# A two-layer encoder trunk: the norms ahead of four matrix products made token tile by token tile

## The reference

```python
def rmsnorm(x, g):
    y = xf * lax.rsqrt(jnp.mean(xf * xf, axis=-1, keepdims=True) + EPS)
    return (y * g.astype(jnp.float32)).astype(x.dtype)
...
    for i in range(DEPTH):
        if i % N_MIXERS == 0:
            x = x + mlstm_mixer(x, *mix_params[i])
        else:
            lambda_init = 0.8 - 0.6 * math.exp(-0.3 * i)
            x = x + diff_attn_mixer(x, positions, *mix_params[i], lambda_init=lambda_init)
        x = x + peer_ffn(x, *ffn_params[i])
```

## Time and profile before

| | |
|---|---|
| median of 3 runs | 1866.83 us (1865.65 to 1868.53) |
| the profiled execution | 1865.97 us, span of its instructions 1864.2 us |
| busy in the span | PE 1847.5 us (99%), DVE 1420.9 (76%), ACT 974.8 (52%), POOL 105.8 (6%) |
| chain that ended last | PE 95%, DVE 3%, ACT 1% |

### The profile page before, as it was taken

How to read it: one execution, slowest core, us unless ns; L and a number is a source line. 1 busy time by engine, 2 the same in 40 slices (tenths; PEclk the granted TensorE clock), 3 DMA queues, 4 the chain that set the end, 5 groups by cost and what they waited for, 6 DMA issues and landing times.

```text
span 1864.2 us, 32895 instructions
## 1 busy us (share of the span) xinstructions
PE 1847.5 (99%) x11242; PEld 1554.4 (83%) x11242; DVE 1420.9 (76%) x2599; ACT 974.8 (52%) x1394; POOL 105.8 (6%) x71
## 2 busy tenths in 40 slices
PE   8999999999999999999999999999999999999999
PEld 6778888888888888888887788888888888888887
DVE  5576688988888888655588757889888888885555
ACT  5475555654545444444467645565545544444443
POOL 0000341000000000000000014410000000000000
PEclk9999999999999999999999999999999999999999
DMA  6345555555555555555553355555555555556555
GB/s 231 135 136 160 162 187 191 181 172 170 167 177 172 180 177 170 193 187 195 192 185 119 115 181 170 182 179 183 180 175 172 180 169 173 176 172 194 198 190 171
DMA packets 89487, 326.15 MB, mean 175 GB/s; under 512 B 10064, under 2 KB 10192, under 8 KB 89040
## 3 DMA queue, kind: packets, MB, share of 16 engines
q1 hardware_dynamic: 88848, 323.00, 53.1%
q10 hardware_dynamic: 576, 2.33, 0.3%
HBM read 324.24 MB, written 1.05 MB: 174 GB/s over the span
## 4 chain that ended last, share of the span: by engine, by line
PE 95%; DVE 3%; ACT 1%; issue 0%; DMA 0%; ACTq 0%; DVEq 0%
PE ps L1531 25%; PE ps L1529 14%; PE ps L1776 13%; PE ps L1778 12%; PE ps L1777 12%; PE ps L1528 4%; PE ps L1724 3%; PE ps L1548 2%; PE ps L1550 2%; PE ps L1549 2%; DVE wl L848 1%; PE ps L1705 1%; PE ps L1668 1%; PE ps L1831 0%; PE ps L1861 0%
## 5 line engine op out<-in xcount | busy, mean ns | idle before, releaser
L848 DVE TENSOR_TENSOR wl<-raw,wh 128x1024 fp32r<-128x1024 f32 x569 | 697.1, 1228 | 158.4 <-ACT wh L477 149.6
L477 ACT ACTIVATE wh<-raw 128x1024 fp32r<-128x1024 f32 x609 | 641.7, 1055 | 312.3 <-PE ps L1778 164.9
L1531 PE MATMUL ps<-hT,wh 128*128 128x512 f32 x2072 | 739.3, 396 | 0.0
L1529 PE MATMUL ps<-hT,wl 128*128 128x256 f32 x2368 | 613.1, 279 | 0.0
L1529 PEld LDWEIGHTS ps<-hT,wl 128*128 128x128 f32 x2368 | 446.6, 189 | 25.1
L1531 PEld LDWEIGHTS ps<-hT,wh 128*128 128x128 f32 x2072 | 389.7, 188 | 79.4
L1776 PE MATMUL ps<-wh,hT 128*128 128x512 f32 x1024 | 402.1, 393 | 0.3 <-DVE big L832 0.2
L1778 PE MATMUL ps<-wh,hT 128*128 128x512 f32 x1024 | 399.2, 390 | 0.0
L1777 PE MATMUL ps<-wl,hT 128*128 128x512 f32 x1024 | 398.6, 389 | 0.0
L1778 PEld LDWEIGHTS ps<-wh,hT 128*128 128x128 f32 x1024 | 192.3, 188 | 40.6
L1776 PEld LDWEIGHTS ps<-wh,hT 128*128 128x128 f32 x1024 | 192.4, 188 | 39.5 <-issue 0.9
(11 more groups left out here) (226 smaller groups left out, 1327.2 us busy)
## 6 DMA issues: line engine op xcount, KB each, us to landing
raw<-stream SPq DMA_DIRECT2D x612, 512.0 KB, 3.5
big<-keys ACTq DMA_DIRECT2D x2, 1024.0 KB, 8.6
x<-x_in SPq DMA_DIRECT2D x1, 1024.0 KB, 5.6
out<-x SPq DMA_DIRECT2D x4, 256.0 KB, 2.1
sm<-small ACTq DMA_DIRECT2D x1, 228.5 KB, 5.8
pos_i<-positions ACTq DMA_DIRECT2D x1, 1.0 KB, 6.7
```

The costliest lines, as they stand in the source:

```text
L477: act.activation(wh[:, r, :], raw[:, r, :], ACT.Copy).then_inc(high_ready, 1)
L848: dve.tensor_tensor(wl[:, r, :], raw[:, r, :], wh[:, r, :].bitcast(F32), ALU.subtract).then_inc(made_low(unit), 1)
L1529: pe.matmul(near, w_l[:, kd, :], hTh[:, kd, :], start=False, stop=False)
L1531: i = pe.matmul(wide, w_h[:, kd, :], both, start=False, stop=(kd == KD - 1))
```

## The change

Five things are changed, the first four in all norms or in those with n > 0.

1. Variance, root and reciprocal are made for each token tile apart, and DVE's adds to x are put between them: both quarters of tile 0, its variance, one quarter of tile 1, reciprocal of tile 0, the other quarter, scaling of tile 0, then tile 1.
2. PE transposes all 8 blocks of tile 0, then all of tile 1, into 4 banks with two blocks in each: blocks kd and kd + 4 share a bank. For tile 1 the transpose of blocks 4 to 7 waits until DVE has made `hTl` of block kd - 4, and ACT's copy of these blocks has the same wait.
3. The warming matmuls ahead of the transposes (10, 16, 10) go; 5 come between the two token tiles for n = 2, 3, 5.
4. Before the feed-forward norms ACT and DVE issue one high and one low part less (`U_WO - 2` for `U_WO - 1`); they come behind the norm.
5. In the loop over 16 softmax steps DVE's call of `ahead` is left out for the last step.

```diff
-        TURN_BANK = {0: (7, 4, 5, 6, 0, 1, 2, 3), 2: (4, 5, 6, 7, 0, 1, 2, 3), 3: (4, 5, 6, 7, 0, 1, 2, 3),
-                     5: (4, 5, 6, 7, 0, 1, 2, 3)}
+        TURN_BANK = {0: (4, 5, 6, 0), 2: (2, 3, 0, 5), 3: (6, 7, 0, 1), 5: (5, 6, 7, 2)}
...
+                def root(t):
+                    act.wait_ge(var_ready, 2 * k + t + 1)
+                    act.activation(rstd[:, t:t + 1], var[:, t:t + 1], ACT.Sqrt).then_inc(std_ready, 1)
...
+                    if i == (2 if n == 0 else 1):
+                        root(0)
+                root(1)
...
+                    if kd >= 4:
+                        act.wait_ge(hT_ready, 8 * n + kd - 3)
...
-            ahead(unit_of["wo0"] + U_WO - 1)
+            ahead(unit_of["wo0"] + U_WO - 2)
...
+            def norm(n, k, add=lambda t, nb: None):
...
+                add(0, 0)
+                add(0, 1)
+                variance(0)
+                add(1, 0)
+                factor(0)
+                add(1, 1)
+                scaled(0)
+                variance(1)
+                factor(1)
+                scaled(1)
...
-                ahead(unit_of["qkv"] + 15 + STEP_AT[j] // 4)
+                if j < 15:
+                    ahead(unit_of["qkv"] + 15 + STEP_AT[j] // 4)
...
-                for kd in range(KD):
-                    for t in range(NT):
+                for t in range(NT):
+                    if t == 1 and n > 0:
+                        keep_warm(4, 5)
+                    for kd in range(KD):
                         if kd in (0, KD // 2):
-                            pe.wait_ge(xn_ready, 4 * XN_TURN[n] + 2 * (kd // 4) + t + 1)
-                        i = pe.transpose(ps[:, TURN_BANK[n][kd], t * P:(t + 1) * P], xn[:, t, kd * P:(kd + 1) * P],
+                            pe.wait_ge(xn_ready, 4 * XN_TURN[n] + 2 * t + kd // 4 + 1)
+                        if t == 1 and kd >= 4:
+                            pe.wait_ge(hT_ready, 8 * n + kd - 3)
...
             def ffn(l):
-                keep_warm(4, 10)
                 transposes((2, 5)[l])
...
-            keep_warm(4, 16)
             transposes(3)
```

More of the change, by code:

```diff
@@ L812, in chain, with variance, factor, scaled @@
                 dve.wait_ge(dve_step, steps[0])
[L814 to L821, removed]
-                    for t in range(NT):
+            def norm(n, k, add=lambda t, nb: None):
+                def variance(t):
+                    dve.wait_ge(ssq_ready, 4 * k + 2 * t + 2)
+                    dve.scalar_tensor_tensor(out=var[:, t:t + 1], in0=ssq[:, t, 0:1], scalar=EPS, in1=ssq[:, t, 1:2],
+                                             op0=ALU.add, op1=ALU.add).then_inc(var_ready, 1)
+                def factor(t):
+                    dve.wait_ge(std_ready, 2 * k + t + 1)
+                    chain(dve.reciprocal(var[:, t:t + 1], rstd[:, t:t + 1]))
+                def scaled(t):
+                    for nb in range(2):
                         half = slice(nb * 512, (nb + 1) * 512)
@@ L864, in gain, with add_to_x @@
                 return lambda kd: sm[:, SM_GAIN + g * KD + kd:SM_GAIN + g * KD + kd + 1]
[L866 to L872, removed]
+            def add_to_x(l, t, nb):
+                last = unit_of[f"wo{l}"] + U_WO - 2 + nb
+                if t == 0:
+                    ahead(unit_of[f"wo{l}"] + U_WO - 2)
+                    dve.wait_ge(wo_mm, 2 * l + nb + 1)
+                else:
+                    dve.wait_ge(used, last + 1)
+                dve.tensor_tensor(x[:, t, nb * 512:(nb + 1) * 512], x[:, t, nb * 512:(nb + 1) * 512],
+                                  ps[:, OUT_BANKS[l][nb] + t, :], ALU.add).then_inc(x_ready, 1)
             def head_var(part, k, scale, eps=None):
@@ L1534, in up_both_halves, with token_half @@
                 i.then_inc(used, 1)
+            def token_half(w, q, t, out, between=lambda t, k: None):
+                w_h, w_l = (v.rearrange("p (k c) -> p k c", k=2) for v in w)
+                for k in range(2):
+                    kd = 2 * q + k
+                    between(t, k)
+                    if t == 0:
+                        tokens_ready(kd)
+                    h_h, h_l = hTh[:, kd, t * P:(t + 1) * P], hTl[:, kd, t * P:(t + 1) * P]
+                    pe.matmul(out, h_h, w_h[:, k, :], start=(kd == 0), stop=False)
+                    pe.matmul(out, h_h, w_l[:, k, :], start=False, stop=False)
+                    i = pe.matmul(out, h_l, w_h[:, k, :], start=False, stop=(kd == KD - 1))
+                return i
             def token_unit(unit, q, out, done, before=lambda t: None, between=lambda t, k: None):
-                w_h, w_l = (w.rearrange("p (k c) -> p k c", k=2) for w in split(unit))
+                w = split(unit)
                 for t in range(NT):
@@ L1541, in token_unit @@
                         before(t)
[L1542 to L1550, removed]
+                    i = token_half(w, q, t, out(t), between)
                     if q == 3 and t == 0:
@@ L1555, in out_projection @@
             def out_projection(l, n, ready):
-                for q in range(4):
+                first = unit_of[f"wo{l}"]
+                for q in range(3):
                     for nb in range(2):
@@ L1781, in down @@
+                        i = down_half(w, r, t, turn is None and r == 0)
                     i.then_inc(used, 1)
```

81 lines of the change are left out of this document (43 added, 38 removed).

## The result

The changed kernel takes 1878.04 us (median of four runs, 1874.13 to 1880.37) beside 1867.09 us for the kernel before (1865.65 to 1868.53). The ratio is 1.0056, with a 95% interval of 1.0042 to 1.0070: it is slower, by some 10.5 us (the medians differ by 10.95; the ratio is not exactly their quotient). The profiled execution is the quickest of the four, 1874.13 us with a span of 1872.2 us, 8.0 us longer than the span of before. This difference between executions, 6 us from the quickest to the slowest, is a part of the answer.

The account below looks back on a forecast made before the run. PE, busy in 99% of the span, was taken as the bound. Terms 0.3 + 1.8 + 3.2 + 1.8 = 7.1 us, plus 1.7 for one clock fall, gave 8.8 us of loss: 1875.6 us, range 1870.5 to 1881.5.

Parts of the forecast that it names:

- the forecast: Main case, 60%: gaps at the norms as worked out, none or one clock fall; 1875.6 us, own range 1872.5 to 1878.5.
- the first rival: Clock falls at two or three of n = 2, 3, 5, staying low through the first query unit: 10.5 to 14.3 us; 27%.
- The sum at full clock: Losses at the four norms added together with the clock at full speed: 7.1 us.
- n = 2: Hand-over at this norm: late second tile and waiting transposes, first query matmul at 144.06; +1.8 us.
- n = 3: Hand-over at this norm: waits plus a low part between hTl blocks, first matmul at 945.07; +3.2 us.
- n = 5: Hand-over at this norm: the same picture as n = 2; +1.8 us.
- n = 0: Norm at the start: hTl hardly moves (12.2), high and low parts come later; +0.3 us.
- The waits: Second tile's transposes of blocks 4 to 7 wait for hTl of blocks 0 to 3, delaying the first matmul after each norm.
- the rival that they are cheap: Copies run ahead of the transposes, so blocks 4 to 7 find their bank free: 3.1 us, 1870; 10%.
- The clock: PE's clock falls to half speed behind the new gaps at n = 2, 3, 5: one fall of three, +1.7 us.
- The last high and low part: Deferred behind the feed-forward norms, ready at about 147.2 before PE wants them at 149.7: no cost.
- The softmax step's call: Call left out at the last of 16 softmax steps asks only for units already requested: 0 us.

Follow-up runs that it names:

- e1: Changed kernel with ten warming matmuls put back ahead of the first transpose of n = 2, 3 and 5: 1874.13 us, 1.0050 of before.
- e9: The changed kernel measured once more, with nothing altered: 1878.96 us, 1.0066 of before.
- e10: Changed kernel with warming put back, plus warming in the holes of n = 2, 3 and 5 and five matmuls at n = 0: 1873.58 us, 1.0034.
- e3: Changed kernel with warming put back, eight banks and no waits for hTl; warming between tiles kept in unused half-banks: 1868.23 us, 1.0015.
- e5: Changed kernel with warming put back ahead of tile 0, eight banks, no waits and no warming between the token tiles: 1.0003 of before.
- e8: Kernel before with n = 0 tile by tile, 12 warming matmuls for 16 at n = 3, last high/low part deferred: 1865.47 us, 0.9994.
- e6: Changed kernel with warming put back, plus warming matmuls in the holes between waiting transposes at n = 2, 3 and 5: 1.0032 of before.
- e7: Changed kernel with warming put back, and at n = 3 DVE's low parts moved behind all eight hTl: 1871.10 us, 1.0027.
- e4: Kernel before with only the four shared banks and the waits for hTl added, at all four norms: 1872.69 us, 1.0046.
- e2: Kernel before without its 10, 16 and 10 warming matmuls, nothing else changed: 1871.21 us, 1.0039.

## Why the prediction came out as it did

The direction was right, and the time lies within the range: 1875.6 us forecast, 1878.04 measured, 8.8 us of loss forecast and some 10.5 measured. It is even within the forecast's own range (1872.5 to 1878.5), by 0.5 us; that is in part luck, since the number of falls was the first rival's and the rest of the loss came out a little under the sum.

**The sum at full clock** (7.1 us) holds within a microsecond or so. With the holes filled the kernel is 1.0032 and 1.0034 of before, 6.0 and 6.3 us (5.05 and 6.35 by the medians). By place: n = 2 1.80 us for 1.8, with the first query matmul at 143.85 for 144.06, in a hand-over that began 0.16 sooner; n = 3 8.17 less 5.13, 3.0 us for 3.2; n = 5 as n = 2 (7.02 us to the first matmul, 7.03 there).

**n = 0** looks mis-sized, and with the wrong sign: +0.3 was the term, and in the first profile the hand-over to n = 2 began 0.16 us sooner than before. But the two profiles are not alike there: that of before had a stretch at half clock at the start, with its transposes in it, and that of the changed kernel had none. hTl began at 11.78, where I had 12.2 and the earlier trace rows have 12.33. Like beside like, the term is about right. With no fall at the start, the hand-over to n = 2 begins at 136.78 to 136.88 with the four banks (changed, e1, e9, e10) and at 136.35 to 136.56 with eight banks and token tile after token tile (e3, e5, e8), 0.2 to 0.5 sooner. With one fall there, it begins at 137.48 and 137.61 (e6, e7) for 136.98 (before), 0.5 to 0.6 later. A fall at the start costs less than the 1.7 us of the others: 0.60 from e10 to e6.

**The waits** are the cause of the loss, against the rival that they are cheap: taking them out gave back 0.92 us at n = 2 and 2.3 at n = 3 (e3), and putting them alone into the kernel before took 1.05 and 2.4 (e4). The low part among the hTl of n = 3 costs 1.1 us of it (e7). The rest is the five warming matmuls, 0.46 us each time (e3 to e5), and the order of the token tiles, 0.3 us each time (e5 beside before). That the order as such costs so little was not said clearly in the prediction; e5, with its ratio of 1.0003, shows it.

**The clock** is the term that was mis-sized. I took one fall of three possible, 1.7 us. The price of one was right (1.6 to 1.67 us). The number wasn't: the changed kernel beside the one with filled holes is 5.4 us slower, which is three such falls or a little more, and its profile there has four. So what the first rival had (two or three falls, 10.5 us and more) is nearer to what the chip does than the forecast's one, and the measured 10.5 and 12.3 us (1.0056 and 1.0066) lie at its lower end. I gave one row for and one against equal weight, and looked at the holes ahead of the transposes. In e1, with these filled, the clock fell behind the sparse transposes of n = 3. A fourth place is the old hole in the softmax, where the earlier trace rows show no fall, but the profiles of e2, e3, e4 and e9 do.

**The parts that cost nothing** came out so. The last high and low part: low parts came at 145.57 and on, and PE waited for none. The softmax step's call issues nothing, and PE's wait there is 2.15 us in the profiles of before and changed.

What stays open: how often each hole brings the clock down, and what decides between the two lengths of the stretches in e6 and e10. Both were seen in single profiles, at most two for one kernel, and what decides in one execution and not in the next was not tried.

## What to carry to other kernels

Price a wait in a chain of transposes by who makes what it waits for, and look at what is queued there among it: a low part that was free while PE worked behind it cost 1.1 us when PE stood ahead of it. Saving PSUM banks by two blocks in each turned a copy that ran behind PE into one that PE waits for. When PE is the bound and a trace shows a hole, add to its length the chance that the clock falls behind it, 1.6 to 1.7 us each here where PE was the bound, and read it from several executions, since one profile can show one fall and the next four. Filler matmuls that end before the wait does cost nothing here (hand-overs of 7.02 and 8.16 us with them and without). And before a step of one or two microseconds is read from two profiles, compare them stretch by stretch: a fall at the start in one of them, or a slower stretch that the change does not touch, gives as much.

## What the runs showed of the hardware

The same instructions with the same holes found the clock at full and at half in different executions, and at different places of one execution: with 2.16 us idle in front at n = 2 it stayed at 1.00 and at n = 3 it was 0.51 (e9). In e1 PE worked on warming matmuls and transposes, with holes of 0.91 and 1.20 us and a few transposes of 128 columns between, before the clock fell. The mean clock of an execution shows that it had falls: 0.999 in the changed kernel's run of 1874.13 us, where the profile has one, and 0.996 in e9's profile with four. It doesn't give the time by itself: the runs with 0.996 took 1876.17, 1879.91 and 1880.37 us.

At the clock's full level a PE-bound stretch of 80 units had two lengths, 241.9 and 243.1 us, in different executions (e6, e10).

The Trainium skill (TensorE: Matmul & The Clock Gate, what's actually happening) says that the clock is set by how busy PE has been of late. In the prediction I had used it as a rule on idleness alone. The fall in e1, with PE at work on and off, agrees with the page's wording and not with my use of it; the softmax's idle stretch, with and without a fall behind it, shows that idle time alone did not decide.
